# A transformer block on one core: the order of weights and x at the start, PSUM banks, selection rounds and filler products in the first stage

## The reference, cut to what matters

```python
a = rmsnorm(h, norm_mix_g)
proj = a @ w_in
q, k, v, iq, ik, iw, z, xbc, dt_raw, gate = jnp.split(proj, offsets, axis=-1)
q, k, iq, ik = (partial_rope(t, positions) for t in (q, k, iq, ik))
# per block of 128 queries
s = relu(einsum('bqhd,bsd->bqhs', iq, ik) * idx_scale)
score = where(causal, einsum('bqhs,bqh->bqs', s, iw * w_scale), -inf)
_, sel = lax.top_k(score, 128)
# softmax attention over the selected, causal keys; 8 heads share 2 key-value heads
merged = sigmoid(gate0) * (attn @ w_attn_branch) + sigmoid(gate1) * (ssd @ w_ssd_branch)
```

## Time and profile before

| | us |
|---|---|
| median of 3 runs | 3402.44 |
| lowest, highest | 3402.29, 3407.26 |
| the profiled execution, its own time | 3403.1 |
| its span in the trace | 3401.0 |
| TensorE busy | 3162.3 (93%) |
| VectorE busy | 1882.6 (55%) |
| ScalarE busy | 1112.5 (33%) |
| GpSimd busy | 1121.2 (33%) |

### The profile page before, as it was taken

One profiled execution on the slowest core, in us unless ns is written; L12 is line 12 of the kernel. 1 busy time (PEld: TensorE's weight loads), 2 busy tenths in 40 slices (PEclk: granted clock), 3 DMA queues, 4 the chain that ended last, 5 costly groups with the idle time before them and its releaser, 6 DMA issues. The chain is left out here.

```text
span 3401.0 us, 38220 instructions
## 1 busy us (share of the span) xinstructions
PE 3162.3 (93%) x14938; PEld 1606.2 (47%) x15208; DVE 1882.6 (55%) x2796; ACT 1112.5 (33%) x1621; POOL 1121.2 (33%) x527
## 2 busy tenths in 40 slices
PE   7779989999979899999999999999998888888997
PEld 3334457444644545555565444444444345433443
DVE  7872557443234484969575155555554863368721
ACT  3234234333323233333333333232333342323221
POOL 3222410233513243342422444444443231224432
PEclk9899999999989999999999999999999987999999
DMA  4211300222412243747466676565663120112321
GB/s 143 74 56 62 106 25 1 81 93 99 130 40 96 81 154 130 211 136 206 147 190 189 201 238 207 199 207 201 203 205 124 63 87 19 50 57 99 100 97 64
DMA packets 264530, 414.14 MB, mean 122 GB/s; under 512 B 147512, under 2 KB 147704, under 8 KB 263968
## 3 DMA queue, kind: packets, MB, share of 16 engines
q1 hardware_dynamic: 264352, 411.69, 37.5%
HBM read 341.55 MB, written 69.22 MB: 121 GB/s over the span
## 5 line engine op out<-in xcount | busy, mean ns | idle before, releaser
L535 POOL TENSOR_TENSOR weights_lo<-weights_as_loaded,weights_hi 128x1024 bf16<-128x1024 f32 x507 | 1119.0, 2209 | 2240.3 <-ACT weights_hi L531 2240.3
L531 ACT ACTIVATE weights_hi<-weights_as_loaded 128x1024 bf16<-128x1024 f32 x507 | 533.3, 1054 | 1221.5 <-PE banks L1873 454.8
L2012 DVE TENSOR_TENSOR activation_lo<-activation_f,activation_hi 128x512 bf16<-128x512 f32 x128 | 277.1, 2165 | 313.0 <-ACT activation_hi L1904 312.9
L1825 PE MATMUL banks<-normed_hi,weights_hi 128*128 128x512 bf16 x991 | 376.3, 380 | 7.3 <-ACT gelu_out L1890 6.1
L1873 PE MATMUL banks<-activation_hi,weights_hi 128*128 128x512 bf16 x1004 | 380.5, 379 | 1.1
L1873 PE MATMUL banks<-activation_hi,weights_lo 128*128 128x512 bf16 x1003 | 380.1, 379 | 1.1
L1873 PE MATMUL banks<-activation_lo,weights_hi 128*128 128x512 bf16 x1003 | 380.1, 379 | 1.1
L1825 PE MATMUL banks<-normed_lo,weights_hi 128*128 128x512 bf16 x999 | 378.5, 379 | 1.8
L1825 PE MATMUL banks<-normed_hi,weights_lo 128*128 128x512 bf16 x1000 | 378.9, 379 | 1.3
L1995 DVE TENSOR_TENSOR one_hot_b<-iota,pick_column 128x1024 bf16<-128x1024 bf16 x64 | 129.8, 2028 | 145.4 <-PE banks L1846 144.1
L1890 ACT ACTIVATE gelu_out<-banks 128x512 f32<-128x512 f32 x128 | 76.2, 595 | 385.2 <-PE banks L1825 377.9
(11 more groups left out here) (479 smaller groups left out, 5209.5 us busy)
## 6 DMA issues: line engine op xcount, KB each, us to landing
weights_as_loaded<-in_u_tiles SPq DMA_DIRECT2D x128, 512.0 KB, 3.8
weights_as_loaded<-in_v_tiles SPq DMA_DIRECT2D x128, 512.0 KB, 3.6
gelu_of_dots<-gelu_out SPq DMA_DIRECT2D x128, 256.0 KB, 2.2
activation_f<-gelu_of_dots SPq DMA_DIRECT2D x128, 256.0 KB, 3.8
expert_weight<-expert_weights SPq DMA_DIRECT2D x128, 256.0 KB, 4.1
expert_weights<-weight_grid_even SPq DMA_DIRECT2D x32, 512.0 KB, 5.9
expert_weights<-weight_grid_odd SPq DMA_DIRECT2D x32, 512.0 KB, 6.5
weights_as_loaded<-in_w_xbc SPq DMA_DIRECT2D x24, 512.0 KB, 3.4
```

Source lines behind the costliest of these rows:

```text
L531: self.nc.scalar.activation(self.whi[:, s, :], self.wraw[:, s, :], ACT.Copy).then_inc(self.w_hi[s], 1)
L535: self.nc.gpsimd.tensor_tensor(self.wlo[:, s, :], self.wraw[:, s, :], self.whi[:, s, :], ALU.subtract).then_inc(self.w_lo[s], 1)
L1825: ins = nc.tensor.matmul(self.ps[:, b, :], u[:, j, k * P:(k + 1) * P], xx[:, k, :], start=k + m == 0, stop=k == DC - 1 and m == 2)
L2012: nc.vector.tensor_tensor(glo[:, j, :], gf[:, j, :], ghi[:, j, :], ALU.subtract).then_inc(S["g_lo"], 1)
```

## The change

What it does, engine by engine:

- SyncE issues weight tile 0 ahead of x, x in pieces of 1, 2, 2 and 3 chunks, weight tile 1 before the last, and the two small tables behind.
- VectorE makes the rests of weight tiles 0 to 3, which GpSimd made. `angles(1)` goes behind them, `angles(0)` goes between the emptying of tiles 0 and 1. ScalarE rounds tile 0 first, and makes the sines of table 0 behind tile 0.
- Tiles take banks n % 4. Small tiles and the column of 1/rms go to bank 4. The index products share banks 5, 6 and 7, and each waits for the relu three before it.
- Block 1's 16 rounds go behind tiles 6 to 12 (2, 2, 2, 3, 2, 3, 2). `select(1)` goes behind the masked scores of unit 0. The rounds of blocks 2 and 3 are spread anew over the units.
- The second filler and the fourth head's scores of the next unit go between the last transposition of a unit and its last `values`. Units 0 to 4 have a second filler, where 0 to 3 and 7 had one.

```diff
-            if u in (0, 1, 2, 3, 7):
+            if u < 5:
                 fill_second[u], f = f, f + 1
...
-        select_between = {0: (2, range(4, 8)), 1: (2, range(8, 12)), 2: (2, range(12, 16)), 3: (3, range(0, 5)), 4: (3, range(5, 10)),
-                          5: (3, range(10, 16))}
+        select_between = {0: ((2, range(4, 9)),), 1: ((2, range(9, 14)),), 2: ((2, range(14, 16)), (3, range(0, 2))),
+                          3: ((3, range(2, 7)),), 4: ((3, range(7, 12)),), 5: ((3, range(12, 16)),)}
+        first_rounds = {6: (0, 2), 7: (2, 4), 8: (4, 6), 9: (6, 9), 10: (9, 11), 11: (11, 14), 12: (14, 16)}
...
-                load_x(0, 2, 0)
+                stream.load(sp, 0)
+                load_x(0, 1, 0)
+                load_x(1, 3, 1)
+                load_x(3, 5, 2)
+                stream.load(sp, 1)
+                load_x(5, 8, 3)
...
-                for u in range(4):
-                    stream.rest(pool, u)
...
                     for h in range(IDX_HEADS):
                         b = (h % 2) * IDX_D
-                        if i > 1:
-                            pe.wait_ge(S["relus"], (i - 2) * IDX_HEADS + h + 1)
-                        nc.tensor.matmul(self.ps[:, 4 + h, 0:(i + 1) * P], QK[b:b + IDX_D, 10 + h // 2, i * P:(i + 1) * P],
+                        n = (i - 1) * IDX_HEADS + h
+                        if n >= 3:
+                            pe.wait_ge(S["relus"], n - 2)
+                        nc.tensor.matmul(self.ps[:, 5 + n % 3, 0:(i + 1) * P], QK[b:b + IDX_D, 10 + h // 2, i * P:(i + 1) * P],
...
-                    if n >= 3:
-                        pe.wait_ge(S["emptied"], n - 2)
-                    products(n, n % 3, raw)
+                    if n >= 4:
+                        pe.wait_ge(S["emptied"], n - 3)
+                    products(n, n % 4, raw)
...
                         if j:
                             values(u, j - 1)
+                    between()
                     values(u, i)
...
-                    attend(u)
-                    if u + 1 < NU:
-                        scores(u + 1, range(3, GRP))
-                    if u in fill_second:
-                        fill(fill_second[u])
+
+                    def between():
+                        if u + 1 < NU:
+                            scores(u + 1, range(3, GRP))
+                        if u in fill_second:
+                            fill(fill_second[u])
+                    attend(u, between)
...
                     copies(u)
+                    if u in fill_second:
+                        take_gate(fill_second[u])
                     if u + 1 < NU:
                         exps(u + 1, range(3, GRP))
...
+                rest(0)
+                for c in range(DC):
+                    split.dve(dve, c)
+                    if c == 4:
+                        rest(1)
+                for c in range(4):
+                    nc.vector.tensor_tensor(squares[:, c, :], self.hT[:, c, :], self.hT[:, c, :], ALU.mult).then_inc(split.squared, 1)
+                rest(2)
+                rest(3)
...
                 for n in range(NQ):
+                    if n == 1:
+                        angles(0)
...
-                    if n >= 8:
-                        largest(1, range(2 * (n - 8), 2 * (n - 7)))
+                    if n in first_rounds:
+                        largest(1, range(*first_rounds[n]))
...
-                largest(1, range(10, 16))
-                select(1)
                 dve.wait_ge(S["roped"], NQ)
                 mask_scores(0, range(GRP))
+                select(1)
                 normalize(0)
```

More of the change, by code:

```diff
@@ L935, in turn_scale @@
                     for t in range(TT):
-                        ins = nc.tensor.matmul(self.ps[:, 3, t:t + 1], self.rs[0:1, t * P:(t + 1) * P], self.ones[0:1, 0:1],
+                        ins = nc.tensor.matmul(self.ps[:, 4, t:t + 1], self.rs[0:1, t * P:(t + 1) * P], self.ones[0:1, 0:1],
                                                start=True, stop=True)
@@ L957, in fill @@
                     elif f == 1:
-                        pe.wait_ge(S["small_taken"], TT)
+                        pe.wait_ge(S["emptied"], NQ - 1)
                     else:
@@ L984, in values, with attend @@
                                      ).then_inc(S["valued"], 1)
-                def attend(u):
+                def attend(u, between):
                     i, c = units[u]
@@ L1062, in take_small @@
                     t = small_order[n]
-                    nc.scalar.activation(small[:, t, :], self.ps[:, 3, 0:292], ACT.Copy, scale=rs_col[:, t:t + 1]
+                    nc.scalar.activation(small[:, t, :], self.ps[:, 4, 0:292], ACT.Copy, scale=rs_col[:, t:t + 1]
                                          ).then_inc(S["small_taken"], 1)
@@ L1070, in relus @@
                         act.wait_ge(S["dots"], (i - 1) * IDX_HEADS + h + 1)
-                        nc.scalar.activation(rel[:, h, 0:(i + 1) * P], self.ps[:, 4 + h, 0:(i + 1) * P], ACT.Relu,
+                        bank = 5 + ((i - 1) * IDX_HEADS + h) % 3
+                        nc.scalar.activation(rel[:, h, 0:(i + 1) * P], self.ps[:, bank, 0:(i + 1) * P], ACT.Relu,
                                              scale=IDX_D ** -0.5).then_inc(S["relus"], 1)
@@ L1126, in _ @@
                 act.wait_ge(self.vecs_in, 16)
+                stream.round(act, 0)
                 for c in range(DC):
[L1128 removed]
+                    act.wait_ge(self.x_in[arrives_with[c]], 16)
                     nc.scalar.activation(raw[0][:, c, :], self.hT[:, c, :], ACT.Copy, scale=self.vec("mix_g", c)).then_inc(split.hi, 1)
[L1130 to L1131 removed]
+                    if c == 4:
+                        stream.round(act, 1)
                 for c in range(4, DC):
@@ L1137, in _, with sines @@
                 act.wait_ge(self.consts_in, 16)
-                for n in (1, 0):
+                def sines(n):
                     act.wait_ge(S["angles"], 2 - n)
@@ L1217, in empty @@
                         dve.wait_ge(swapped[n % 2], swap_count(n - 2))
-                    nc.vector.tensor_tensor(halves[p, n % 2, :], self.ps[p, n % 3, :], table[p, at + 1, :], ALU.mult)
-                    nc.vector.tensor_tensor(QK[:, c, :], self.ps[:, n % 3, :], table[:, at, :], ALU.mult).then_inc(S["emptied"], 1)
+                    nc.vector.tensor_tensor(halves[p, n % 2, :], self.ps[p, n % 4, :], table[p, at + 1, :], ALU.mult)
+                    nc.vector.tensor_tensor(QK[:, c, :], self.ps[:, n % 4, :], table[:, at, :], ALU.mult).then_inc(S["emptied"], 1)
                 def rope(n):
@@ L1337, in _, with rest @@
                 link(nc.vector.memset(zero[:, :], 0.0))
+                def rest(u):
+                    dve.wait_ge(self.w_hi[stream.slot(u)], stream.use(u) + 1)
+                    nc.vector.tensor_tensor(self.wlo[:, u, :], self.wraw[:, u, :], self.whi[:, u, :], ALU.subtract
+                                            ).then_inc(self.w_lo[stream.slot(u)], 1)
+                rest(0)
+                for c in range(DC):
+                    split.dve(dve, c)
+                    if c == 4:
+                        rest(1)
[3 more added lines that the diff above has]
+                rest(3)
                 dve.wait_ge(S["positions"], 16)
@@ L1341, in _ @@
                 angles(1)
-                for c in range(DC):
-                    dve.wait_ge(self.x_in[c // 2], 16)
-                    split.dve(dve, c)
-                    if c >= 4:
-                        nc.vector.tensor_tensor(squares[:, c - 4, :], self.hT[:, c - 4, :], self.hT[:, c - 4, :], ALU.mult
-                                                ).then_inc(split.squared, 1)
-                angles(0)
                 dve.wait_ge(self.consts_in, 16)
@@ L1378, in select_more @@
                 def select_more(u):
-                    i, rounds = select_between[u]
-                    largest(i, rounds)
-                    if rounds[-1] == N_SEL // 8 - 1:
-                        select(i)
+                    for i, rounds in select_between[u]:
+                        largest(i, rounds)
+                        if rounds[-1] == N_SEL // 8 - 1:
+                            select(i)
                 for u in range(NU):
```

21 lines of the change are left out of this document (7 added, 14 removed).

## The result

The changed kernel takes 3412.27 us (median of 16 runs, 3408.59 to 3413.26); the kernel before takes 3404.03 in 16 runs of the same job. The ratio is 1.0022, with a 95% interval of 1.0015 to 1.003: **slower by 8 us**. The forecast was 3397.6 with a range up to 3404, so sign and range are both wrong.

What follows compares the result with a forecast made beforehand. VectorE was taken to bound 103.2 to 146.5 us, and TensorE with some 25 us of waits the eight units. Gains of 1.4 up to the first scores and 3.4 in the units made 4.8: 3397.6 us, range 3387 to 3404.

Steps and rivals of the forecast that it cites:

- Up to the first scores: From tile 10's end to unit 0's scores: TensorE and VectorE finish together, scores end at 145.1 instead of 146.5, gain 1.4.
- six rope and rest passes of 0.7 to 2: Part of VectorE's 21.1 us queue before the first scores, beside 7 rounds, the weighing of block 3 and three banks.
- the step before: The index products of block 3 end at 116.45 instead of 103.2, and tile 10 ends at 123.35.
- the term for the clock: TensorE at half clock behind a long idle time: 1.7 us lost for each long wait, ends 0 and 3.4.
- Net gain 3.4: The eight attention units: 8.4 us of waits removed, 5.0 added.
- 1.3 of half clock: In the units' first filler: 1.3 us saved, as the wait ahead of it becomes short.
- new waits at third scores: In units 1, 2, 3, 4 and 6, third head's scores wait for a bank behind the masked scores: 3.4 us added.
- moving unit 7's second filler to unit 4 costs nothing and brings nothing: In the eight units: this move was given no effect on the time.
- Here is what the change costs: Three banks for four index products: waits of 1.5, 3.85 and 8.0, together 13.35, with half clock 16.75 us.
- The front gain: Rival: index product waits are short and the early start is kept, total gain 13.8, 3388.6 us; chance 0.20.
- The start: Rival: first matmul no more than 4.6 us earlier, since weights and x share transfers, 3400.8 us; chance 0.13.
- The slow one: Rival: in units 0 to 4 the selection makes stores late, 3 us in each of five units, 3412.6; chance 0.07.

Runs made afterwards that it cites:

- Experiment 12: Changed kernel with the rests of three weight tiles moved from GpSimd into VectorE's queue behind tiles 10, 11 and 12: 3404.7 us, ratio 1.0005 to the kernel before.
- experiment 1: Changed kernel with four banks for the index products again, q tiles on three banks, small tiles on bank 3: 3393.82 us, ratio 0.9972 to the kernel before.
- experiment 4: Changed kernel with the second filler and fourth head's scores back behind the last `values`, fillers still in units 0 to 4: 3402.08 us, ratio 0.9992.
- Experiment 5: Changed kernel with four index banks again and the fillers back behind the last `values`: 3384.23 us, ratio 0.9944 to the kernel before.
- experiment 11: Changed kernel with the last second filler back in unit 7 instead of unit 4, still ahead of the last `values`: 3411.06 us, ratio 1.0016.
- experiment 3: Changed kernel, three index banks kept, with ScalarE making a block's relus ahead of `again.act` instead of behind it: 3395.64 us, ratio 0.9979.
- experiment 9: Experiment 5 with ScalarE copying the 1/rms column ahead of `again.act(0)` and `angles(0)` straight behind `angles(1)`: 3376.65 us, ratio 0.9911 to the kernel before.

## Why the prediction was wrong

**The step that failed** is "Up to the first scores", in the sentence "21.1, so the end of both falls together". The queue of VectorE took 25.0. The mis-sized term is "six rope and rest passes of 0.7 to 2": in my sum they had some 5.4 (21.1 less the 7, 4.9 and 3.75 of the others), and they took 9.6 (0.67, 2.60, 1.64, 1.54, 0.68, 2.48), plus 0.65 of idle time for a DMA between them. So the scores ended at 151.2 and not at 145.1: 6.1 of the miss. Experiment 12 shows the cause, since less GpSimd beside more VectorE work made the same stretch 4 us shorter.

The price was there to be read. In the kernel before, the same six passes behind tile 10 already take 10.1 us:

```profile
113.90 2.01 DVE L1226 TENSOR_TENSOR q_k_iq_ik<-q_k_iq_ik,halves_swapped 32x512 f32<-32x512 f32 x1
115.84 2.60 DVE L221 TENSOR_TENSOR normed_lo<-few_chunks,normed_hi 128x512 bf16<-128x512 f32 x1
...
126.49 1.94 DVE L1226 TENSOR_TENSOR q_k_iq_ik<-q_k_iq_ik,halves_swapped 32x512 f32<-32x512 f32 x1
...
131.51 2.09 DVE L1226 TENSOR_TENSOR q_k_iq_ik<-q_k_iq_ik,halves_swapped 32x512 f32<-32x512 f32 x1
...
135.48 1.48 DVE L1226 TENSOR_TENSOR q_k_iq_ik<-q_k_iq_ik,halves_swapped 32x512 f32<-32x512 f32 x2
```

So the passes beside GpSimd's rests explain why the forecast missed, and not why the new kernel is slower than the old one: that is the index banks and the place of the fillers (experiments 1, 4 and 5).

The queue also began 1.7 later than the 123.35 of the step before, though small tile 0 started 1.5 earlier than summed. From small tile 0 to the first matmul behind the last index product TensorE takes 67.4 us (50.44 to 117.87) where it took 47.8 (55.40 to 103.21): 19.6 more, and my sum has 16.75 there (1.7 + 13.35 + 1.7). The waits were 1.0 shorter than summed, but the term for the clock was too small. Behind the waits of 3.51 and 7.58 the granted clock is 0.50 up to 96 and up to 120 us and 0.62 and 0.65 in the two microseconds after, so the half level lasts an estimated 4.8 and 5.5 us and costs 2.4 and 2.8, not 1.7. What is left is the fourth product of each block, which now runs alone behind its wait (0.70, 1.64 and 2.07 us).

The rule that I cited belongs here. The Trainium skill, "SBUF — State Buffer", section "SBUF: two separate sides", says that of a VectorE pass with two SBUF inputs and a GpSimd pass that reads SBUF, whoever starts first keeps the shared ports for its whole instruction and blocks the other. For the small weights the trace agrees: with VectorE first, 2.58 us for the 2336 columns that took 4.09 before, and GpSimd's rest beside it 3.47 instead of 2.12. But I used the rule for this one pass, where it made the change cheaper, and did not apply it to a row of short passes, each of which is short beside a rest of 2.12 us. There the trace agrees too: each late pass ends 0.54 to 0.55 us behind the rest that it met.

**The second step that failed** is "Net gain 3.4" for the units; they came out at 147.2, as before. The "1.3 of half clock" was not saved: behind the unforeseen 4.04 filler 2 took 7.6 us instead of 5.2. The new waits at third scores made 4.1 instead of 3.4, unit 5's copy wait 10.33 instead of some 9.7, and unit 7's grew from 2.99 to 3.84. The sentence "moving unit 7's second filler to unit 4 costs nothing and brings nothing" is true only with the fillers ahead of the values (experiment 11). What the new order loses against the same filler behind the values, 10.2 us by experiment 4's medians and 8.1 by the traces of the units, stands nowhere in my sum, because I did not follow `store(4)` back to the values.

**The rest.** The third part is 1.9 us behind the units, in the same code (3109.2 against 3107.3). Experiment 5 has 3107.1 there, experiment 3 3105.8 and experiment 1 3109.2, so I take it for scatter. 6.1 + 3.4 + 1.9 = 11.4 is the miss in the span (6.6 later where 4.8 earlier was forecast). The medians miss by 14.7: the kernel before had 3404.03 beside the kernel after and not 3402.44, which is 1.6, and the other 1.7 lie between the profiled executions and the medians.

**What was right.** The first matmul is 1.3 earlier than forecast, a gain of 9.1 us, 0.3 above the higher of its ends (4.6 and 8.8): ScalarE began to round the weights at 5.46, VectorE's rest took 1.23 against "about 1.3". `angles(0)` lasted 5.9 us (37.34 to 43.26), as forecast, 4.11 of them for its multiply-adds with one rest beside them. The waits at the index products came within 0.4 us each, so "Here is what the change costs" was right in mechanism, and its 16.75 was some 3 us too low, as said above. Taking it back gives 18.5 by the medians (experiment 1). The 3.0 us that the selection was to give in unit 5 came: alone, it takes the copy wait from 12.71 to 9.7.

**None of the rivals happened.** The front gain was not kept, for the index waits stood. The start came earlier, not later. The slow one named the right mechanism, two-input passes beside a rest, at the wrong place: it looked for it in the units, where a store would be late, and gave it 0.07. In the units no store was late by it; the same mechanism struck ahead of unit 0, where VectorE was without slack by my own sum. That this rival's 3412.6 lies beside the measured 3412.27 is chance. A sum in which two engines arrive together has its whole uncertainty on the slow side, and the range had none of it.

## What to carry to other kernels

Where two engines are forecast to arrive together, price each shared-port pass beside the other engine's instructions from the timeline, one by one; lateness of either counts in full, and behind it comes the half clock. A buffer taken from one stage for another has to be priced at its longest holder, here the bank that waits for a relu in an in-order queue behind three engines; where that consumer stands in its queue was worth most of what the buffer was (experiment 3). Filler work belongs behind the product that the other engine's next long piece hangs on, not ahead of it: here the copy wait of unit 5 was 10.33 with the filler ahead and 4.49 with it behind.

## What I had not expected of the hardware

- Moving three rests to the busier engine made that engine's queue shorter (25.0 to 21.0 us with 3.6 us added), as its passes went from 2.60 and 1.64 to 0.67.
- Behind a wait of 4.04 us TensorE ran at the 1.2 GHz level: 7.6 us for a filler of 5.2. Behind the same wait of 1.26 us it kept 2.4 GHz in the kernel after and fell to 1.2 in experiment 11 (granted clock 1.00 and 0.50 from 76 to 78 us).
- Executions of one kernel differ by some 6 us: experiment 11 has 3405.2 twice and some 3411 eight times, experiment 9 has 3370.5 once and 3376 to 3379 three times. The traces place part of it behind the units (3100.2 to 3111.4 us for the same code). What it is, no run here shows; four runs don't settle a difference of 0.1%.
